# Start and end of a twelve-stage fp32 kernel: the first loads one after the other, products of ones ahead of the first product, the last product and store by column halves

## The reference

```python
for i in range(4):                       # first block
    h = h + rmsnorm(mixer_i(rmsnorm(h, gains[i, 0])), gains[i, 1])
    h = h + rmsnorm(sq_relu_mlp(rmsnorm(h, gains[i, 2]), w_up[i], w_down[i]), gains[i, 3])
for layer in range(2):                   # second block
    x = x + attention_layer(x)
    x = x + square(relu(rms_norm(x, gain) @ w_up)) @ w_down
```

## Time and profile before

| | |
|---|---|
| median of three runs | 2264.4 us |
| the profiled execution's own time | 2263.4 us |
| its span, first to last instruction | 2261.5 us |
| PE busy | 2206.3 us, 98% |
| DVE busy | 1482.9 us, 66% |
| ACT busy | 1204.9 us, 53% |
| POOL busy | 223.7 us, 10% |
| DMA | 368.93 MB, mean 163 GB/s |
| mean granted clock of TensorE | 0.988 |

### The profile page before, as it was taken

One profiled execution on the slowest core, in us unless ns is written; L12 is line 12 of the kernel. 1 busy time (PEld: TensorE's weight loads), 2 busy tenths in 40 slices (PEclk: granted clock), 3 DMA queues, 4 the chain that ended last, 5 costly groups with the idle time before them and its releaser, 6 DMA issues.

```text
span 2261.5 us, 29454 instructions
## 1 busy us (share of the span) xinstructions
PE 2206.3 (98%) x11632; PEld 1867.2 (83%) x11632; DVE 1482.9 (66%) x2070; ACT 1204.9 (53%) x1828; POOL 223.7 (10%) x204
## 2 busy tenths in 40 slices
PE   7999999999999999999999999988999999999999
PEld 7878888988888878889778888767888888798887
DVE  6645755897556667657636666886665898465655
ACT  5555544756445655455555444656445565455443
POOL 0000000662000020000001000001000000162000
PEclk9999999999999999999999999989999999899999
DMA  7534656615555436555544755523655766302653
GB/s 256 186 130 149 200 191 193 176 44 160 194 192 177 146 98 210 193 194 177 168 149 155 209 188 186 170 91 107 205 186 168 204 173 187 112 1 94 194 194 115
DMA packets 201528, 368.93 MB, mean 163 GB/s; under 512 B 6943, under 2 KB 142495, under 8 KB 201392
## 3 DMA queue, kind: packets, MB, share of 16 engines
q1 hardware_dynamic: 197776, 358.70, 48.8%
q0 software_dynamic: 3616, 8.35, 2.1%
HBM read 365.97 MB, written 1.05 MB: 162 GB/s over the span
## 4 chain that ended last, share of the span: by engine, by line
PE 91%; DVE 4%; ACT 2%; POOL 1%; issue 1%; DMA 0%; DVEq 0%; SPq 0%; ACTq 0%
PE PS L666 47%; PE PS L787 14%; PE PS L784 6%; PE PS L771 6%; PE PS L822 2%; PE PS L981 2%; PE PS L1327 2%; PE PS L1296 1%; PE PS L902 1%; DVE wlo L1953 1%; PE PS L829 1%; PE PS L1072 1%; PE PS L786 1%; POOL wlo L2836 1%; PE PS L1311 1%
## 5 line engine op out<-in xcount | busy, mean ns | idle before, releaser
L1953 DVE TENSOR_TENSOR wlo<-raw,whi 128x1024 fp32r<-128x1024 f32 x658 | 791.4, 1229 | 190.2 <-ACT whi L1382 189.4
L1382 ACT ACTIVATE whi<-raw 128x1024 fp32r<-128x1024 f32 x680 | 699.6, 1054 | 376.9 <-PE PS L666 312.7
L666 PE MATMUL PS<-whi,U 128*128 128x512 f32 x1728 | 486.9, 398 | 7.6 <-DVE U L2722 1.5
L787 PE MATMUL PS<-U,whi 128*128 128x512 f32 x1344 | 474.4, 397 | 0.0
L666 PEld LDWEIGHTS PS<-whi,U 128*128 128x128 f32 x1728 | 324.5, 190 | 81.7 <-issue 13.7
L784 PE MATMUL PS<-U,wlo 128*128 128x256 f32 x1176 | 330.0, 281 | 0.0
L787 PEld LDWEIGHTS PS<-U,whi 128*128 128x128 f32 x1344 | 247.0, 188 | 48.5
L666 PE MATMUL PS<-wlo,U 128*128 128x512 f32 x864 | 269.3, 393 | 0.0
L2072 DVE TENSOR_TENSOR AR<-PS,AR 128x512 f32<-128x512 f32 x96 | 66.3, 691 | 309.3 <-ACT AR L1468 309.3
L666 PE MATMUL PS<-whi,fH 128*128 128x512 f32 x832 | 258.2, 392 | 0.9 <-DVE fL L2210 0.9
L666 PE MATMUL PS<-whi,fL 128*128 128x512 f32 x832 | 256.3, 389 | 0.0
(11 more groups left out here) (326 smaller groups left out, 2413.4 us busy)
## 6 DMA issues: line engine op xcount, KB each, us to landing
raw<-in_mlp_w_up SPq DMA_DIRECT2D x64, 1024.0 KB, 5.5
raw<-in_mlp_w_down SPq DMA_DIRECT2D x64, 1024.0 KB, 5.0
raw<-in_ret_w_in SPq DMA_DIRECT2D x48, 1024.0 KB, 5.3
raw<-in_m_w_up SPq DMA_DIRECT2D x32, 1024.0 KB, 5.6
raw<-in_m_w_down SPq DMA_DIRECT2D x32, 1024.0 KB, 5.0
raw<-in_kv_w SPq DMA_DIRECT2D x24, 1024.0 KB, 5.3
raw<-in_ret_w_out SPq DMA_DIRECT2D x16, 1024.0 KB, 4.9
raw<-in_gla_w_in SPq DMA_DIRECT2D x12, 1024.0 KB, 5.2
```

The source lines that it names most:

```text
L666: mm = e.matmul(bank(b + nb), a, w[:, nb * 512:(nb + 1) * 512], start=(begins and n < 2), stop=(ends and n >= 4))
L787: mm = e.matmul(o, w_h[:, k, :], U[:, k, :, :, :], start=(k == 0), stop=(k == 7))
L1382: e.activation(split_half(whi, i, x), raw_halves(i)[x], ACT.Copy).then_inc(HI.tick((i, x)), 1)
L1953: e.tensor_tensor(split_half(wlo, i, x), a, split_half(whi, i, x).bitcast(F32), ALU.subtract).then_inc(LO.tick((i, x)), 1)
```

## The change

The order of the first loads: the second rows of x are issued when chunk 0 has landed, and chunk 1 when the second rows have landed. PE multiplies `ones` by `ones` (128 x 128, fp32, into bank 3, which nobody reads) ten times before the first transposes and 17 times after them. In the last MLP the rows tt = 1 are multiplied for all four k in the left column half first, then in the right one; DVE adds the left half behind a signal of its own (`TOP[S, "left"]`), and every column half is stored by a DMA of its own, 256 KB.

```diff
--- before.py
+++ after.py
@@ -313,6 +313,8 @@
             if S == DIL:
                 gemms += [(S, n) for n in range(9)]
             gemms.append((S, "y"))
+
+        gemms.append((LAST, "left"))
 
         TOP = Event(sem("s_top_rows"), gemms)
         last_chunk = {}
@@ -705,7 +707,7 @@
 
 
                 i0 = first[S + 1] - 2
-                for tt in range(2):
+                for tt in range(2 if S != LAST else 1):
                     for c in range(2):
                         for k2 in range(2):
                             i, k = i0 + c, 2 * c + k2
@@ -726,6 +728,22 @@
                             if (tt, k) == (1, 2) and S != LAST:
                                 turn_in(S + 1, 0)
 
+                if S == LAST:
+
+                    for nb in range(2):
+                        n = slice(nb * 512, nb * 512 + 512)
+                        for k in range(4):
+                            i, k2 = i0 + k // 2, k % 2
+                            w_h, w_l = split_half(whi, i, k2), split_half(wlo, i, k2)
+                            a_h, a_l = ap(k, 1)
+                            e.matmul(bank(2 + nb), a_h, w_h[:, n], start=False, stop=False)
+                            e.matmul(bank(2 + nb), a_h, w_l[:, n], start=False, stop=False)
+                            mm = e.matmul(bank(2 + nb), a_l, w_h[:, n], start=False, stop=(k == 3))
+                            if nb == 1:
+                                mm.then_inc(USED.tick((i, k2)), 1)
+                        if nb == 0:
+                            mm.then_inc(TOP.tick((S, "left")), 1)
+
             def turn_quarter(t, tt, j, src):
 
                 for kk in range(4):
@@ -1351,8 +1369,16 @@
             turn_free[MLP4] = [AOL[3], AO[3], MASKED[DIFF, 7]]
             turn_free[MLP5] = [MASKED[DIL, 15, 0], LOL[15]]
 
+            def keep_busy(n):
+
+                for _ in range(n):
+                    e.matmul(PS[:, 3 * 512:3 * 512 + 128], ones[:, :], ones[:, :], start=True, stop=True)
+
+            e.wait_ge(*ONES[0])
+            keep_busy(10)
             e.wait_ge(*s_id[1])
             turn_in(RET0, 0)
+            keep_busy(17)
             pe_ret(RET0)
             pe_mlp(MLP0)
             pe_conv(CONV)
@@ -2023,8 +2049,8 @@
                                            ALU.mult, ALU.add).then_inc(HN.tick((S + 1, tt, j)), 1)
 
             def add_plain(S, tt):
-                e.wait_ge(*rows_done((S, "y"), tt))
                 for j in range(2):
+                    e.wait_ge(*(TOP[S, "left"] if (S, tt, j) == (LAST, 1, 0) else rows_done((S, "y"), tt)))
                     c = slice(512 * j, 512 * j + 512)
                     if S in MLPS:
                         ins = e.scalar_tensor_tensor(h[:, tt, c], bank(2 * tt + j), st[:, 24 + tt:25 + tt], h[:, tt, c],
@@ -2995,16 +3021,18 @@
             e.dma_start(ident[:, :], d["ident"]).then_inc(s_id.sem, 16)
             load_x(0)
             load_chunk(0)
+
+            e.wait_ge(*landed(0))
             load_x(1)
-
-            e.wait_ge(*landed(0))
+            e.wait_ge(*s_x[1][1])
             for i in range(1, NCH):
                 load_chunk(i)
             for tt in range(2):
                 for j in range(2):
                     e.wait_ge(*HN[LAST + 1, tt, j])
-                e.dma_start(out[0, tt * 128:tt * 128 + 128, :], h[:, tt, :]).then_inc(s_out, 16)
-            e.wait_ge(s_out, 32)
+                    c = slice(512 * j, 512 * j + 512)
+                    e.dma_start(out[0, tt * 128:tt * 128 + 128, c], h[:, tt, c]).then_inc(s_out, 16)
+            e.wait_ge(s_out, 64)
 
         with nc.Block() as block:
             @block.sync
```

## The result

The changed kernel takes 2270.49 us, the median of nine runs (2268.47 to 2273.0), against 2264.39 for the kernel before (2263.53 to 2265.43): a ratio of 1.0026, 95% interval 1.0017 to 1.0035. It is slower by 6.1 us; 2270.3 was forecast.

A forecast was written before the change was run, and what follows sets the result against it. PE bounds the kernel, with 91% of the chain of waits. Chunk 1's lateness +5.2, slow clock +2.0 and column halves -1.3 make +5.9 us: 2270.3 us forecast, range 2264.2 to 2272.6.

The forecast's parts named there:

- The collision: At the start, chunk 1, issued 2.9 us later, shares with POOL's loads; PE goes on at 25.4, 5.2 us later.
- Both conditions that the prediction named: At the start: chunk 1 meets POOL's 1.5 MB, and ACT makes chunk 1's high halves before the second rows' U.
- they stand behind it, and I take the gain as 0: First loads on SP's queue: x's second rows do not delay chunk 0, which lands at 10.4, at the earliest 8.4.
- The prediction's own mark: At the start: the forecast is wrong if chunk 0 lands before 9.5, or if ACT has chunk 1 before 20.
- x's second rows: Their 512 KB load on SP's queue was to take 2.9 us to landing, so chunk 1 is issued at 13.3.
- The clock behind the wait: The second rows' product starts at 1.2 GHz after PE's idle time: 2.0 us lost, bounds 0 and 3.
- The ones: Products of ones before the first rows' product: booked 0, worth 1.6 us if chunk 1 were not late.
- The halves: Last product, addition and store by column halves: 1.3 us saved, bounds 0.7 and 1.6.
- The later stages: Rival, 7%: the clock's falls in the attention stages move too, 1 or 2 us either way, up to 2273.
- 52, a third of 12, and 7: Chances of slower by over 0.2%: most of the forecast's 60, the chunk-0-helped rival (2268.3, 12%), and the later-stages rival (7%).

The follow-up runs named there:

- experiment 3: The changed kernel, but POOL's 1.5 MB of loads wait for chunk 1 in place of chunk 0: 2265.13 us, ratio 1.0005.
- experiment 5: The changed kernel, but ACT makes U of x's second rows ahead of chunk 1's high halves: 2263.57 us, ratio 0.9999.
- experiment 2: The changed kernel with the old order of the first loads, products of ones and column halves kept: 2261.57 us, ratio 0.9987.
- experiment 1: The kernel before with only the new order of the first loads, no products of ones and no column halves: 2271.41 us, ratio 1.0032.
- experiment 6: The changed kernel with 44 more products of ones ahead of the second rows' product: 2268.14 us, ratio 1.0018.
- experiment 4: The changed kernel without SP's wait for x's second rows, chunk 1 issued right behind them: 2268.49 us, ratio 1.0018.
- 8: The kernel before with only the products of ones, ten before the first transposes and 17 behind them: 2263.02 us, ratio 0.9996.
- experiment 9: The changed kernel without SP's wait for x's second rows, ACT's order swapped, POOL's 1.5 MB waiting for chunk 1: 2259.70 us, ratio 0.9982.
- 7: The kernel before with only the last product, addition and store by column halves: 2263.01 us, ratio 0.9997.
- experiment 10: The mended kernel of experiment 9, but x's second rows issued right behind chunk 0 again, without waiting for its landing: 2261.05 us, ratio 0.9988.

## Why the prediction was right, and where it was not

**The collision: right in kind and size, by errors that cancel.** The forecast had ACT take chunk 1 at 22.0 and PE go on at 25.4. The loads' order alone gave 22.03 and 25.33. Taking POOL's loads away gave back 5.4 us (experiment 3), swapping ACT's order 6.9 (5). Both conditions that the prediction named are needed for the full loss: with either one mended the time is near that of before, and 3.6 or 2.0 us are left of the 8.9 against experiment 2.

The match of 22.03 with 22.0 is luck: in experiment 1 chunk 0 came 1.3 us earlier than I had it, x's second rows took 0.8 us longer and chunk 1 0.5. So is a part of the match in the time, 2270.49 against 2270.3, for the nine executions reach over 4.5 us, and the profiled one lost 9.2 us at the start where I had 7.2.

But chunk 0 did not land at 10.4. The step "they stand behind it, and I take the gain as 0" failed: with x's second rows behind chunk 0 it is taken at 9.65 to 10.38 us (five profiles, before among them), without them at 8.5 to 9.1 (seven). The prediction had drawn from the order in one ring that chunk 0 is not helped by taking away what stands behind it; the runs decide otherwise. The prediction's own mark, wrong if chunk 0 lands before 9.5, was met by the start and not by the time, for chunk 1 then took longer: 9.2 us from its issue in experiment 1 and 11.4 in the changed kernel's profile, where I had 8.7.

From the earlier trace rows I had let it go on beside POOL's loads at 0.81 MB in 6.5 us; in fact it got 0.01 MB in its first 4 us. Then it had chunks 2 and 3 beside it, where I had counted all that SP's queue moves as chunk 1's: from chunk 1's issue to its landing SP's queue moved 2.31 MB, and 1.69 to 1.99 in experiments 1, 5 and 6. The rows read were those of a queue already running; chunk 1's data came up against one that had begun before it. That happened in all four profiles in which chunk 1 was issued into POOL's burst (the changed kernel's and those of experiments 1, 5 and 6): SP's first packet came 3.4 to 4.0 us after the issue. With the engines idle, in experiment 3, it came 1.0 us after. In experiment 4 and in the kernel before, where SP's data was already moving, the two queues took turns, packet for packet. Why a load that comes second gets nothing for so long I have not tested.

The Trainium skill's page DMA: Bandwidth & Descriptors, section Queues, rings and completion order, has each engine take turns between the queues it has work for. The equal numbers of packets, 238 and 238 in before, agree with it; the 1.0% against 91.5% of the changed kernel's first stretch do not, unless chunk 1's work had not reached the engines. The same section says that completion is not first in, first out per issuing engine, and with that the 2.29 MB agree.

**x's second rows.** 3.4 us to landing in the changed kernel's profile and 3.7 in experiment 1, where I took 2.9 from the last store.

**The clock behind the wait.** Booked at 2.0; 2.35 by experiment 6, and 2.3 in the profile (6.25 against 3.94 us).

**The ones.** Booked at 0 while chunk 1 is late: right, for PE had finished the first rows' product by 15.4 and then waited. Without that lateness I had 1.6, and 1.1 behind ACT; the ones alone gave 1.1 by the medians, within the interval. In the profiles the second rows' product began 1.9 us earlier than in before, 0.4 of it from chunk 0's landing. Their duration was within the bounds: 4.47 us for ten, mostly slow, and 3.96 for seventeen at the full clock.

**The halves.** 1.3 booked, 1.3 in the profiles (4.5 to 3.2 us) and 1.2 by the medians, the latter within the interval. The store became 0.6 us shorter, the addition 0.7.

**The later stages** were a rival at 1 or 2 us. The profiled execution had 1.8 of it. By the starts of the same ACT instructions before and behind it, DIFF was longer by 1.0 to 1.7 us in the profiles of experiments 1 to 4, 8 and 9 too, and by 0.1 at most in those of 5, 6, 7 and 10; the stage is the same in all of them. DIL did the like: 1.7 us longer in the profiles of 7 and 10, by 0.3 at most in the others. I can't say what decides it; that it belongs to the execution and not to the change is likely but not shown; the changed kernel's nine times reach from 2268.47 to 2273.0.

**The chances.** By the prediction's own parts (52, a third of 12, and 7) slower by over 0.2% adds up to 63%, not 62%.

## What to carry to other kernels

A load that is put off does not move alone: list what other queues start at the same event, and ask which transfer now comes behind which. When a landing becomes late, the loss is set by the first engine that waits for it in its program order; work queued behind it that needs nothing from it should stand ahead. Matmuls that keep the clock up are worth something only next to the product they are for: the 17 of the change gave nothing to the product behind the long wait, and 44 inside that wait gave it 2.3 us.

## What was not expected of the hardware

- A transfer behind another in the same queue slows the one ahead: 1.35 us in the time (experiment 10 against 9) and 0.5 to 1.9 us in the landing of 1 MB over twelve profiles.
- A load issued shortly after another queue's 1.5 MB had begun to move sent its first packet 3.4 to 4.0 us after its issue in four profiles, against 1.0 us with the engines idle (experiment 3). In the changed kernel 2.29 MB of its queue passed before its own 1.05 MB was complete: the bytes of one queue do not move strictly in the order of the issues.
- Where both queues were moving data, they moved packets in equal number (238 and 238 from 17 to 20 us in before, 243 and 238 from 14.5 to 17.5 in experiment 4), so the queue with the smaller packets got 0.24 MB and the other 0.87.
- The clock was at half after a wait of PE of 4.37 us (experiment 3) and stayed up over one of 1.06 us (experiment 9). In between it went either way: it stayed up over 2.30 us before the first product of experiment 10 and fell 1.1 us after the end of one of 2.46 us in experiment 5. What decides it these runs don't show.
